# Two hardware loops over layers become written-out code in a two-model transformer kernel on one core

## What is computed

```python
for l in range(DEPTH):                      # DEPTH = 2, first_block; second_block has the same frame
    mod = (c_act @ w_ada[l] + b_ada[l]).reshape(B, N_MOD, D_MODEL)
    h = modulate(rms_norm(x, norm_gain[l, 0]), mod[:, 0], mod[:, 1])
    x = x + 0.5 * mod[:, 2] * swiglu(h, ffn_w_gate[l, 0], ffn_w_up[l, 0], ffn_w_down[l, 0])
    h = modulate(rms_norm(x, norm_gain[l, 1]), mod[:, 3], mod[:, 4])
    x = x + mod[:, 5] * hybrid_mixer(h, ...)   # first: two attentions and a pooling; second: dilated attention and a convolution
    h = modulate(rms_norm(x, norm_gain[l, 2]), mod[:, 6], mod[:, 7])
    x = x + 0.5 * mod[:, 8] * swiglu(h, ffn_w_gate[l, 1], ffn_w_up[l, 1], ffn_w_down[l, 1])
```

## Time and profile before

| | us |
|---|---|
| median of 3 runs | 3083.66 |
| lowest and highest of the 3 | 3079.17, 3085.49 |
| span of the profiled execution, first to last instruction | 3078.6 |
| PE busy in it | 2966.8 (96%) |
| PE weight loads busy | 2866.8 (93%) |
| DVE busy | 2104.4 (68%) |
| ACT busy | 1268.0 (41%) |
| POOL busy | 4.8 (0%) |
| mean granted TensorE clock | 0.977 of full |

### The profile page before, as it was taken

The page is one execution under the profiler, slowest core; times in us unless marked ns, Lnnn a source line. Parts: engine busy times, 40 slices in busy tenths (PEclk is TensorE's granted clock), DMA queues, the critical chain, the costliest instruction groups (busy, mean ns, idle before and its releaser), DMA issues.

```text
span 3078.6 us, 59148 instructions
## 1 busy us (share of the span) xinstructions
PE 2966.8 (96%) x23231; PEld 2866.8 (93%) x23231; DVE 2104.4 (68%) x2869; ACT 1268.0 (41%) x1500; POOL 4.8 (0%) x28
## 2 busy tenths in 40 slices
PE   6999999999899999999999999999999999999998
PEld 5999988999899998899999999889989999998998
DVE  6767755876766775776776776567667677656766
ACT  2434335433334434543443443454334343345433
POOL 0000000000000000000000000000000000000000
PEclk9999989999899998999999999999999999999999
DMA  8776742576687662467677667536766766753674
GB/s 285 239 252 229 225 143 98 183 261 215 204 276 252 221 204 89 154 220 242 225 232 232 212 223 234 178 108 224 231 218 218 232 212 225 234 190 104 227 232 164
DMA packets 534450, 642.48 MB, mean 209 GB/s; under 512 B 12571, under 2 KB 500579, under 8 KB 534275
## 3 DMA queue, kind: packets, MB, share of 16 engines
q1 hardware_dynamic: 521151, 628.18, 62.3%
q10 hardware_dynamic: 13124, 11.93, 1.3%
HBM read 638.95 MB, written 8.97 MB: 210 GB/s over the span
## 4 chain that ended last, share of the span: by engine, by line
PE 89%; DVE 5%; issue 3%; ACT 2%; DMA 1%; DVEq 0%; SPq 0%; ACTq 0%
PE pair L1169 19%; PE pair L1170 18%; PE pair L1171 18%; PE acc L1169 8%; PE acc L1171 8%; PE acc L1170 8%; PE acc L1328 2%; PE small L1369 2%; PE stat L1248 2%; PE small L1241 2%; DVE temp L937 1%; DVE rstd L805 1%; ACT w_high L444 1%; DVE w_low L758 1%; PE small L1231 1%
## 5 line engine op out<-in xcount | busy, mean ns | idle before, releaser
L1169 PE MATMUL pair<-h_high,w_high 128*128 128x256 f32 x4480 | 1295.7, 289 | 17.1 <-DVE h_low L812 12.9
L758 DVE TENSOR_TENSOR w_low<-raw,w_high 128x2048 fp32r<-128x2048 f32 x433 | 990.2, 2290 | 467.5 <-ACT w_high L444 466.7
L1170 PE MATMUL pair<-h_low,w_high 128*128 128x256 f32 x4480 | 1280.1, 286 | 0.0
L1171 PE MATMUL pair<-h_high,w_low 128*128 128x256 f32 x4480 | 1279.8, 286 | 0.0
L444 ACT ACTIVATE w_high<-raw 128x2048 fp32r<-128x2048 f32 x434 | 826.5, 1906 | 293.6 <-PE acc L1171 256.1
L1169 PEld LDWEIGHTS pair<-h_high,w_high 128*128 128x128 f32 x4480 | 872.8, 195 | 27.9 <-issue 27.4
L1170 PEld LDWEIGHTS pair<-h_low,w_high 128*128 128x128 f32 x4480 | 873.3, 195 | 0.0
L1171 PEld LDWEIGHTS pair<-h_high,w_low 128*128 128x128 f32 x4480 | 872.2, 195 | 0.0
L1169 PE MATMUL acc<-y_high,w_high 128*128 128x256 f32 x1792 | 510.0, 285 | 4.0 <-DVE y_low L908 4.0
L775 DVE SCALAR_TENSOR_TENSOR ada_raw<-ada_raw,now 128x256 f32<-128x256 f32 x1008 | 488.8, 485 | 36.0
L1171 PE MATMUL acc<-y_high,w_low 128*128 128x256 f32 x1792 | 508.5, 284 | 0.0
(11 more groups left out here) (165 smaller groups left out, 2398.2 us busy)
## 6 DMA issues: line engine op xcount, KB each, us to landing
ada_raw<-in_w_ada_all SPq DMA_DIRECT2D x150, 1024.0 KB, 7.4
raw<-in_w_in SPq DMA_DIRECT2D x128, 1024.0 KB, 5.3
raw<-in_ffn_gate_all SPq DMA_DIRECT2D x89, 1024.0 KB, 5.4
raw<-in_ffn_up_all SPq DMA_DIRECT2D x89, 1024.0 KB, 5.4
raw<-in_ffn_down_all SPq DMA_DIRECT2D x88, 1024.0 KB, 5.3
raw<-in_w_branch SPq DMA_DIRECT2D x12, 1024.0 KB, 5.0
raw<-in_w_out SPq DMA_DIRECT2D x8, 1024.0 KB, 4.9
raw<-in_w_conv_out SPq DMA_DIRECT2D x8, 1024.0 KB, 5.0
```

Source lines behind the costliest of these rows:

```text
L758: nc.vector.tensor_tensor(w_low[:, slot, :], raw[:, slot, :], w_high[:, slot, :].bitcast(F32), ALU.subtract).then_inc(w_low_ready.sem, 1)
L1169: mm(dst, a_h, b_h, start=start, stop=False, skip_group_check=True)
L1170: mm(dst, a_h, b_l, start=False, stop=False, skip_group_check=True)
L1171: return mm(dst, a_l, b_h, start=False, stop=True, skip_group_check=True)
```

## The change

On each of the five engines, the hardware loop over the layers of a stack becomes a Python loop. Each stack's layer body now stands in the program twice. Every count, tile offset and DRAM address that held the layer's register becomes a constant, or, in the inner FFN loop, a constant plus the part that hangs on `r`. Which instructions compute, on what data, in what order on each engine, and for which event each waits, stays as it was.

```diff
@@ sync @@
             for b in range(2):
-                with sp.Fori(0, DEPTH) as l:
+                for l in range(DEPTH):
                     at = (b, l)
@@ scalar @@
             for b in range(2):
-                with act.Fori(0, DEPTH) as l:
+                for l in range(DEPTH):
                     at = (b, l)
@@ gpsimd @@
             for b in range(2):
-                with pool.Fori(0, DEPTH) as l:
+                for l in range(DEPTH):
                     at = (b, l)
@@ vector @@
             for b in range(2):
-                with dve.Fori(0, DEPTH) as l:
+                for l in range(DEPTH):
                     at = (b, l)
@@ tensor @@
             for b in range(2):
-                with pe.Fori(0, DEPTH) as l:
+                for l in range(DEPTH):
                     at = (b, l)
```

## The result

| | before | after |
|---|---|---|
| median, us | 3083.94 (4 runs) | 3058.72 (4 runs) |
| lowest to highest, us | 3079.17 to 3085.49 | 3057.26 to 3060.27 |
| profiled span, us | 3078.6 | 3058.4 |
| mean granted TensorE clock | 0.977 | 0.980 |

The ratio of after to before is 0.9924, with a 95% interval of 0.991 to 0.9938. It is faster by 25.2 us between the first medians, 20.2 us between the two profiled spans, and 22.5 us between the means of all runs of the study (3083.4 over 47 runs of before, 3060.9 over 14 of after). The forecast was 3064.2 us, with a range of 3054 to 3074.

A forecast was written before the change was run, and what follows sets the result against it. PE, busy 96% of the span, was taken as the bound, leaving only its 111.8 us idle to win. Back edges 18.1 plus registers 0.7 and 0.7 made 19.5 us, so 3083.66 - 19.5 = 3064.2 us, range 3054 to 3074.

The forecast's parts named there:

- Step 1: At the two loop-backs, removing the taken back edges saves 18.1 us, priced by the boundary between the stacks.
- What is late next: At the former loop-backs, PE is next held by squares, root, rstd and first remainder, as at every norm: 9.06 us.
- Step 2: Removing the layer's registers saves 0.7 us at three layer boundaries and 0.7 us in the mixers' heads.
- The upper end: In 48 mixer heads, three handoffs each with one 0.04 us register instruction on the path would give 5.8 us.
- Step 3: DMAs keep number, sizes and order, and code executed once is fetched once: cost zero, at most 5.7 us if exposed.
- About the same bytes: Sign expected in the profile of after: the instruction queues move about the same bytes as before.
- A: Inner loops begin to wait for code, up to 5.7 us per taken edge; two such loops give 3109.8 us; chance 4%.
- B: At the new seams the wait for code stays: 3082.3 us, or 3073 with one seam of two; chance 4%.
- C: Registers across the kernel cost more than their rows show: another 20 us of "issue" goes, 3044 us; chance 6%.

The follow-up runs named there:

- e2: Changed kernel, but each engine keeps the layer's number in a register, set by one move per written-out layer: 3067.92 us, ratio to before 0.9941.
- e3: Kernel before, hardware loops and registers kept, with a prefetch hint on each engine's outer back edge: 3073.12 us, ratio to before 0.9962.
- e10: Second measurement of e2, the changed kernel with the layer's number in a register on each engine: 3065.44 us, ratio to before 0.9939.
- e12: Changed kernel with six chained copies holding ACT ahead of layer 1's first square in each stack, no branch: 3075.22 us, ratio to before 0.9976.
- e11: Changed kernel, but DVE alone keeps the layer's number in a register: 3063.94 us, ratio to before 0.9931.
- e4: Changed kernel with the inner loops written out too, no hardware loop left: 3061.67 us, ratio to before 0.9934.
- e7: Changed kernel, but PE alone keeps its hardware loop over the layers: 3068.16 us, ratio to before 0.9956.
- e5: Changed kernel, but ACT alone keeps its hardware loop over the layers: 3081.27 us, ratio to before 0.9994.

## Why the prediction was right

**The bound and the place.** PE's full trips stayed at 35.44 us, and the gain came where the idle time had been, at the two loop-backs. e2 takes away the taken edge alone and has all but 0.10 us of each seam's gain; e3 leaves the edge and takes away the fetch.

**Step 1, the two back edges, 18.1 us.** The profile of after gives 17.5 in the same four stages, e2 and e10 give 18.1 over whole runs, with a standard error of 1.5, so that the same figure came out is in part luck. Taking the boundary between the stacks as the price of a boundary without a jump was what made this close. Its parts hold as well: 5.7 us of fetch (0.42 with a hint), 2.7 us of slower squares (2.6 in e12). "What is late next", 9.06 us, came out as 8.82, since the end of the loop (0.14) and the registers between ACT's copy and square (0.10) went too.

**Step 2, the registers, 0.7 + 0.7 us.** The boundary between the stacks gave 0.24 us (9.06 to 8.82), as taken, but only 0.10 of it is registers, and the two former seams gave 0.10 each (e2): 0.4 in all where 0.7 was taken. In the heads the 0.7 was too small: the heads of stack 1 gave 0.13 us each, 1.9 us over 14 intervals (e11). The step took the chain shares of DVEq and ACTq (0%) as its measure, but a register instruction that delays a wait's answer shows there as idle time with another releaser, as the 0.78 us before L937 did. The upper end, 5.8, had covered it. In whole runs the registers are worth 4.4 us with a standard error of 1.6, and the rows account for 2.2 (three boundaries at 0.10 and the heads); the other 2.2 stay open and are within the scatter.

**The time itself** was forecast 5.5 us too high. Some 2 us of this are the draw: the first four runs of after have a median of 3058.72, all 14 a mean of 3060.9. Between the means the gain is 22.5 us and not 19.5. The mis-sized term is the registers (1.4 taken; 2.3 seen in the rows, 4.4 in the runs). The two profiled spans show only 20.2 us because that of before was itself 3 us early.

**Step 3** held: the DMAs' own bytes are the same, and less code is fetched, not more, as the register instructions went: with them kept (e2) the two instruction queues move 1.82 and 0.46 MB, without them 1.79 and 0.29. "About the same bytes" was thus not quite right for the second queue.

**The rivals.** A (inner loops begin to wait): each program is longer, but no trip takes over 35.44 us and e4 shows the inner edges to be free. B (the wait stays): no issue piece is left at either seam. C (registers much dearer): right in direction alone, at 2.3 to 4.4 us and far from 20. It took "issue" as time that could be won; e10 keeps 2.2% of it (after has 1.2%) at a profiled span only 0.9 us longer.

## What to carry to other kernels

A hardware loop costs this kernel nothing while no code has to be fetched again at its back edge, as in the inner loops here; where the body is so long that its head is gone, each taken back edge stalls that engine for the fetch of the head (5.7 us here), and what the kernel pays is the worst engine's part, not the sum. Price such an edge by a boundary of the same work that is passed without a jump. To get rid of it, write the outer loop out, or hint the edge, which brought half of the gain at no growth of the code; and allow for a stall of the matmul engine costing more than its length, since the clock can fall with it (2.6 us on top of 5.4 in e12, nothing in the squares after 3.15 us in e3).

## What was not expected of the hardware

- The fetch behind ACT's taken edge takes the same 5.7 us whether several engines fetch at once or ACT alone (5.75 and 5.70 us of idle time).
- With the hint, ACT's wait behind the branch was 0.42 us at the first seam, yet PE stood 3.15 us there; the hint was not equally good on every engine and edge.
- How slow the squares were did not hang only on how long PE had stood before them: after 3.15 us idle they took 3.72 us (e3), after 4.61 us 5.29 (e7), after 5.97 and 6.43 us 6.35 and 6.43 us (e12). But in e5 they took 6.39 us at the first seam and 5.13 at the second, after 6.38 and 6.39 us idle; what else decides is not shown.
- One program's executions differ by up to 15 us (3056.42 to 3071.51 for the variant with registers) at mean granted clocks from 0.973 to 0.982; the 14 of the changed kernel stay within 9.2 us (3057.26 to 3066.48).
